# Paged sample attention: two groups of pages in flight, K and V pages requested in alternating runs of four

## The reference: what is computed

```
def fox_sample(k_past, v_past, logf_past, q, k, v, logf):
    ...
    s_past = jnp.einsum('bqhd,bkhd->bhqk', q, k_past).astype(F32) * scale + g[..., :, None] + suffix[..., None, :]
    s_new = jnp.einsum('bqhd,bkhd->bhqk', q, k).astype(F32) * scale + g[..., :, None] - g[..., None, :]
    ...
    p = jax.nn.softmax(jnp.concatenate([s_past, s_new], axis=-1), axis=-1).astype(v.dtype)
    return (jnp.einsum('bhqk,bkhd->bqhd', p[..., :n_past], v_past)
            + jnp.einsum('bhqk,bkhd->bqhd', p[..., n_past:], v))
```

## Time and profile before

| | |
|---|---|
| median of three executions | 2553.26 us (2551.98 to 2556.07) |
| profiled execution | 2555.88 us, span 2554.0 us |
| busy in the span | PE 2039.9 us, PEld 1529.0, DVE 1094.5, ACT 321.0, POOL 197.4 |
| DMA over the span | 320.44 MB, mean 125 GB/s |
| mean granted TensorE clock | 0.886 of full speed |

### The profile page before, as it was taken

The page is one execution under the profiler, slowest core; times in us unless marked ns, Lnnn a source line. Parts: engine busy times, 40 slices in busy tenths (PEclk is TensorE's granted clock), DMA queues, the critical chain, the costliest instruction groups (busy, mean ns, idle before and its releaser), DMA issues.

```text
span 2554.0 us, 41115 instructions
## 1 busy us (share of the span) xinstructions
PE 2039.9 (80%) x16723; PEld 1529.0 (60%) x16723; DVE 1094.5 (43%) x1979; ACT 321.0 (13%) x785; POOL 197.4 (8%) x266
## 2 busy tenths in 40 slices
PE   6998865455555555555899999999999889999996
PEld 4776643333333333334677777777777667777774
DVE  4323644444444444445443344533234543335443
ACT  2003520000000000000112210011110111220002
POOL 1003100000000000000100012220000110002221
PEclk9998987777667677677999999999999899999998
DMA  4121037677676777764111221231110111212211
GB/s 145 66 95 61 1 127 254 243 241 255 224 257 224 246 246 243 248 237 162 66 66 66 73 93 66 82 114 35 66 68 28 51 66 69 97 66 75 91 66 37
DMA packets 127992, 320.44 MB, mean 125 GB/s; under 512 B 10236, under 2 KB 10514, under 8 KB 127678
## 3 DMA queue, kind: packets, MB, share of 16 engines
q1 hardware_dynamic: 124258, 304.67, 33.8%
q0 software_dynamic: 3296, 12.98, 1.5%
q10 hardware_dynamic: 252, 0.16, 0.0%
HBM read 309.20 MB, written 8.55 MB: 124 GB/s over the span
## 4 chain that ended last, share of the span: by engine, by line
PE 78%; DVE 17%; ACT 2%; issue 2%; DMA 0%; DVEq 0%; ACTq 0%; SPq 0%
PE ps L852 44%; DVE work L1879 9%; PE ps L1052 8%; PE ps L1074 5%; PE ps L1149 2%; PE ps L1150 2%; PE ps L1062 2%; DVE stats L1894 2%; ACT work L1450 2%; PE ps L774 1%; PE ps L775 1%; PE ps L1001 1%; PE ps L803 1%; PE ps L804 1%; DVE work L1904 1%
## 5 line engine op out<-in xcount | busy, mean ns | idle before, releaser
L1052 PE MATMUL ps<-work,big 32*32 32x256 f32 x6144 | 191.7, 556 | 256.5 <-DVE work L1879 252.7
L1052 PEld LDWEIGHTS ps<-work,big 32*32 32x32 f32 x6144 | 133.8, 129 | 312.8 <-DVE work L1879 266.5
L852 PE MATMUL ps<-xn,wring 128*128 128x288 f32 x1104 | 295.8, 412 | 20.0 <-DVE xn L1598 15.7
L852 PE MATMUL ps<-work 128*128 128x288 f32 x1152 | 296.4, 411 | 11.9 <-DVE work L1645 7.8
L852 PEld LDWEIGHTS ps<-work 128*128 128x128 f32 x1152 | 222.0, 193 | 75.0 <-issue 12.8
L852 PEld LDWEIGHTS ps<-xn,wring 128*128 128x128 f32 x1104 | 212.1, 192 | 80.6 <-issue 20.1
L852 PE MATMUL ps<-big,wring 128*128 128x288 f32 x944 | 252.8, 412 | 7.6 <-DVE big L2142 7.6
L1879 DVE STREAM_TRANSPOSE work<-work 128x768 f32<-128x768 f32 x256 | 222.5, 935 | 0.0
L852 PEld LDWEIGHTS ps<-big,wring 128*128 128x128 f32 x944 | 182.2, 193 | 59.4 <-DVE big L2142 8.5
L1672 DVE TENSOR_TENSOR work<-ps,work 128x288 f32<-128x288 f32 x72 | 32.9, 457 | 320.5 <-PE ps L852 320.5
L707 POOL TENSOR_TENSOR h<-h,xn 128x288 f32<-128x288 f32 x96 | 106.0, 1107 | 812.6 <-DVE xn L1679 698.1
(11 more groups left out here) (348 smaller groups left out, 2507.9 us busy)
## 6 DMA issues: line engine op xcount, KB each, us to landing
work<-in_cache_k SPq DMA_DIRECT2D x256, 384.0 KB, 5.6
big<-in_cache_v SPq DMA_DIRECT2D x256, 384.0 KB, 5.4
wring<-in_w_up SPq DMA_DIRECT2D x16, 2048.0 KB, 7.5
wring<-in_w_down SPq DMA_DIRECT2D x16, 2048.0 KB, 7.9
wring<-in_w_in_odd SPq DMA_DIRECT2D x6, 2048.0 KB, 8.0
wring<-in_w_in_even SPq DMA_DIRECT2D x5, 2048.0 KB, 13.8
wring<-in_w_out_even SPq DMA_DIRECT2D x2, 2048.0 KB, 7.9
wring<-in_w_out_odd SPq DMA_DIRECT2D x2, 2048.0 KB, 7.9
```

The costliest lines, as they stand in the source:

```text
L852: last = mm(bank, w[:, k, :], x[:, k, :], start=k == 0 and not onto, stop=k == 3, skip_group_check=onto)
L1052: last = mm(ps[32 * c:32 * c + 32, 4 + q, 0:256], w, x, start=(n == 0), stop=(n == 2 * HC))
```

## The change

The work of a group is unchanged; its order on the engines, one PSUM area and the engine of one copy are not.

- SP requests K pages 0 to 7, and from there on runs of four K pages and four V pages in turn: K pages n to n+3, then V pages n-8 to n-5. The page numbers of both runs are read ahead of the K run. What each request waits for is the same as before.
- PE scores group g, then weighs pages 4 to 7 of group g-1, turns the probabilities of group g with eight transposes in a row (`turn_probs`), and weighs pages 0 to 3 of group g. The turned probabilities go to columns 256 to 511 of banks 4 to 7, beside the scores.
- ACT takes all eight turned tiles to SBUF with one copy of 128x1024 (`take_probs`), in place of DVE's two copies of 128x512.
- DVE turns the K pages of group g+1 while group g is worked on: three of them, then the shift of group g, one more, `add_out` of group g-1, the bias, and the last four.
- The new tokens' steps are split (`score_new`, `turn_new`, `weigh_new` on PE; `shift_new`, `take_new`, `start_out` on DVE) and spread over two groups; they and the turned output have areas of their own in bank 2. The counters `turn_taken` and its formulas are gone; the row sum and the decay have two slots, by the group's parity.

The diff, cut to its core:

```diff
         shift_s = lambda b, n: stat(b, 2 + n % 2)
-        den_s, group_den, decay, group_max, rec_s = (lambda b, n=n: stat(b, n) for n in (4, 5, 6, 7, 8))
+        den_s, group_max, rec_s = (lambda b, n=n: stat(b, n) for n in (4, 7, 8))
+        group_den, decay = (lambda g, n=n: stat(g // GS, n + 4 * (g % 2)) for n in (5, 6))
         c1 = work[:, 0:I["tab1"].shape[1]]
         O1 = I["tab1"].shape[1]
...
+        new_psum = ps[:, 2, 0:192]
+        out_psum = ps[:, 2, 192:448]
...
-            for g in range(NG):
-                for n in range(g * GP, (g + 1) * GP):
...
+            def k_page(n, page):
+                if n == 8:
+                    sp.wait_ge(sem("pool_d_ready"), 1)
+                if n >= KSLOTS:
+                    sp.wait_ge(sem("scored"), (n - KSLOTS) // GP + 1)
+                sp.dma_start(k_ring[:, k_slot(n), :], rows_of("cache_k", page)).then_inc(k_in[k_slot(n)], 16)
+            def v_page(n, page):
+                if n >= VSLOTS:
+                    sp.wait_ge(sem("v_page_used"), n - VSLOTS + 1)
+                sp.dma_start(v_ring[:, n % VSLOTS, :], rows_of("cache_v", page)).then_inc(v_in[n % VSLOTS], 16)
+            for n in range(0, GP, 4):
+                ids = page_ids(n)
+                for m in range(4):
+                    k_page(n + m, ids[m])
+            for n in range(GP, NB * PAGES, 4):
+                k_ids, v_ids = page_ids(n), page_ids(n - GP)
+                for m in range(4):
+                    k_page(n + m, k_ids[m])
+                for m in range(4):
+                    v_page(n - GP + m, v_ids[m])
+            for n in range(NB * PAGES - GP, NB * PAGES, 4):
+                ids = page_ids(n)
+                for m in range(4):
+                    v_page(n + m, ids[m])
...
-            def turn_half(g, u):
-                if u == 0:
-                    pe.wait_ge(sem("exp_done"), g + 1)
-                pe.wait_ge(sem("turn_taken"), turns_before_group(g) + u)
-                for m in range(4):
-                    at = place(g, 4 * u + m) * P
-                    last = tr(ps[:, 2, m * P:(m + 1) * P], probs[:, at:at + P], ident)
+            def turn_probs(g):
+                pe.wait_ge(sem("exp_done"), g + 1)
+                if g:
+                    pe.wait_ge(sem("probs_in"), g)
+                for at in range(GP):
+                    last = tr(ps[:, 4 + at // 2, 256 + at % 2 * P:256 + at % 2 * P + P], probs[:, at * P:at * P + P],
+                              ident)
                 last.then_inc(sem("probs_turned_s"), 1)
             def weigh_page(g, p):
                 n = g * GP + p
-                if p % 4 == 0:
-                    pe.wait_ge(sem("probs_in"), 2 * g + p // 4 + 1)
                 if p == 0:
-                    pe.wait_ge(sem("out_added"), outs_before_group(g))
+                    pe.wait_ge(sem("probs_in"), g + 1)
+                    if g:
+                        pe.wait_ge(sem("out_added"), g)
                 pe.wait_ge(v_in[n % VSLOTS], 16 * (n // VSLOTS + 1))
...
+            def score_new(b):
...
-                pe.wait_ge(sem("turn_taken"), turns_before_new(b))
+                if b:
+                    pe.wait_ge(sem("new_added"), b)
...
+            def turn_new(b):
...
+            def weigh_new(b):
...
             def turn_out(b):
...
+                if b:
+                    pe.wait_ge(sem("outputs_placed"), b)
+                tr(out_psum[:, 0:P], ostage[:, 0:P], ident)
+                tr(out_psum[0:D, P:2 * P], ostage[:, P:HC * D], ident).then_inc(sem("out_turned"), 1)
-            new_tokens(0)
+            score_new(0)
+            turn_new(0)
+            weigh_new(0)
             for g in range(NG):
+                b, new = g // GS, g // GS + 1
                 score_group(g)
-                if g % GS == 0 and g:
-                    turn_out(g // GS - 1)
-                for u in range(2):
-                    turn_half(g, u)
-                for p in range(GP):
+                if g:
+                    for p in range(GP // 2, GP):
+                        weigh_page(g - 1, p)
+                if g % GS == GS - 1 and new < NB:
+                    weigh_new(new)
+                turn_probs(g)
+                if g % GS == GS - 2 and new < NB:
+                    score_new(new)
+                for p in range(GP // 2):
                     weigh_page(g, p)
-                if g % GS == GS - 2 and g // GS + 1 < NB:
-                    new_tokens(g // GS + 1)
+                if g % GS == GS - 2 and new < NB:
+                    turn_new(new)
+                if g % GS == 0 and b:
+                    turn_out(b - 1)
+            for p in range(GP // 2, GP):
+                weigh_page(NG - 1, p)
             turn_out(NB - 1)
...
                 act.wait_ge(sem("shift_made"), g + 1)
                 if g:
-                    act.wait_ge(sem("probs_turned_s"), 2 * g)
+                    act.wait_ge(sem("probs_turned_s"), g)
                 act_f(probs.rearrange("p (g q k) -> p q g k", g=GP, q=4),
                       ps[:, 4:8, 0:256].rearrange("p q (g k) -> p q g k", g=GP), ACT.Exp,
-                      bias=shift_s(b, n), accum_out=group_den(b)).then_inc(sem("exp_done"), 1)
-                act_f(decay(b), shift_s(b, n - 1), ACT.Exp, bias=shift_s(b, n), scale=-1.0)\
+                      bias=shift_s(b, n), accum_out=group_den(g)).then_inc(sem("exp_done"), 1)
+                act_f(decay(g), shift_s(b, n - 1), ACT.Exp, bias=shift_s(b, n), scale=-1.0)\
...
+            def take_probs(g):
+                act.wait_ge(sem("probs_turned_s"), g + 1)
+                act_f(pTs.rearrange("p (a g) r -> p a (g r)", g=2), ps[:, 4:8, 256:512], ACT.Copy)\
+                    .then_inc(sem("probs_in"), 1)
             exp_new(0)
             for g in range(NG):
                 exp_group(g)
...
-            def take_half(g, u):
...
             def add_out(g):
                 b = g // GS
                 dve.wait_ge(sem("decay_made"), g + 1)
-                own(stt(den_s(b), den_s(b), decay(b), group_den(b), ALU.mult, ALU.add))
+                own(stt(den_s(b), den_s(b), decay(g), group_den(g), ALU.mult, ALU.add))
                 dve.wait_ge(sem("v_page_used"), GP * (g + 1))
-                dve.wait_ge(sem("out_added"), outs_before_group(g))
+                dve.wait_ge(sem("out_added"), g)
                 o = out_acc[:, b % 2, :]
-                stt(o, o, decay(b), ps[:, 3, 0:HC * D], ALU.mult, ALU.add).then_inc(sem("out_added"), 1)
...
+            def shift_new(b):
...
+            def take_new(b):
...
+            def start_out(b):
...
+            def turn_pages(g, pages):
+                if g < NG:
+                    for p in pages:
+                        turn_page(g * GP + p)
+            stage_queries(0)
+            shift_new(0)
+            take_new(0)
+            start_out(0)
+            turn_bias(0)
+            turn_pages(0, range(GP))
             for g in range(NG):
-                turn_bias(g)
-                for p in range(GP):
-                    turn_page(g * GP + p)
-                if g % GS == 0 and g:
-                    place_out(g // GS - 1)
+                b, new = g // GS, g // GS + 1
+                with_new = new < NB
+                if g % GS == GS - 2 and with_new:
+                    stage_queries(new)
+                turn_pages(g + 1, range(0, 3))
                 shift_group(g)
-                for u in range(2):
-                    take_half(g, u)
-                add_out(g)
-                if g % GS == GS - 1:
-                    scale_out(g // GS)
-                if g % GS == GS - 2 and g // GS + 1 < NB:
-                    new_tokens(g // GS + 1)
+                turn_pages(g + 1, range(3, 4))
+                if g:
+                    add_out(g - 1)
+                if g % GS == 0 and b:
+                    scale_out(b - 1)
+                if g % GS == GS - 1 and with_new:
+                    start_out(new)
+                if g + 1 < NG:
+                    turn_bias(g + 1)
+                if g % GS == GS - 2 and with_new:
+                    shift_new(new)
+                turn_pages(g + 1, range(4, 6))
+                if g % GS == GS - 2 and with_new:
+                    take_new(new)
+                turn_pages(g + 1, range(6, 8))
+                if g % GS == 0 and b:
+                    place_out(b - 1)
+            add_out(NG - 1)
+            scale_out(NB - 1)
```

More of the change, by code:

```diff
@@ L548, in rows_of @@
                 return I[cache][0, bass.ds(page, 1)].rearrange("o p h d -> (o p) (h d)")
-            for g in range(NG):
-                for n in range(g * GP, (g + 1) * GP):
-                    if n % 4 == 0:
-                        ids = page_ids(n)
-                    if n == 8:
-                        sp.wait_ge(sem("pool_d_ready"), 1)
-                    if n >= KSLOTS:
-                        sp.wait_ge(sem("scored"), (n - KSLOTS) // GP + 1)
```

(24 more changed lines are left out.)

44 lines of the change are left out of this document (8 added, 36 removed).

## The result

The changed kernel takes 2295.28 us (median of 4; 2289.08 to 2297.59), the kernel before beside it 2554.0 us. The ratio is 0.898 (95% interval 0.896 to 0.900), 259 us less. The forecast was 2278 us, within 2238 to 2350.

The account below looks back on a forecast made before the run. A chain of waits through one group was taken to bound the kernel. 31 steps of 17.0 us in place of 803.3 us save 276.3, plus 1 at the end, less 2.6 to the median: 2278 us, range 2238 to 2350.

Parts of the forecast that it names:

- What bounds the kernel: Sample attention: engines half busy, each waiting for the one ahead in the same group; 803.3 us for 31 steps, 25.91 each.
- Transfers, 15.7 us: Page transfers of one group: 6.29 MB at the 399 to 411 GB/s seen with full queues, 15.7 us.
- The rival that took 350 GB/s from the share: Page transfers: sustained rate below the burst, 350 GB/s at a full DMA share, 18.0 us a group; chance 0.24.
- PE's path, 14.9 us: PE in one group: 13.2 us busy, 0.4 exposed before turned tiles, 1.3 for ACT's copy and handoffs; 14.9 us.
- The request chain, 15.5 to 17.3 us: From one group's scores through requesting, landing and transposing the next K pages to its scores: 15.5 us, 17.3 with loaded queue.
- The sum, 17.0 us: One step of the loop: five paths side by side holding each other up, between 15.7 and 18.8 us, taken as 17.0.
- The allowance of 1.3 us above the transfers: Step of the loop: 1.3 us added to 15.7 us because the paths leave no room for each other's jitter.
- Starved PE: PE in scoring: instructions arrive late over the full DMA engines, 2.2 us a group more, step 19.2 us, 2346 us; chance 0.18.
- Transfers alone: Step of the loop: nothing but page transfers counts, 15.7 us a step, 2238 us; chance 0.12.
- the serial ring: SP's request order makes the loop serial again, 27.8 us a step, 2613 us; chance 0.04, including an overlap not coming about.

Follow-up runs that it names:

- the transfers almost alone: Changed kernel without K transposes (one column copied), scoring 32 of 112 products a group, weighing one product in most pages; all requests and waits kept: 2234.5 us.
- SP's old order: Changed kernel with all 8 K pages of a group requested, then all 8 V pages, compute order new: 2619.6 us, 1.027 of the kernel before.

## Why the prediction was right, point by point

**What bounds the kernel.** A chain through one group, with the stage's 803 us as all that can change: right. 265.7 of 266.8 us come from the stage.

**Transfers, 15.7 us.** 15.8 us at 397 GB/s with the transfers almost alone. The Trainium skill's page "DMA: Bandwidth & Descriptors", section Specifications, has 358 GB/s for a core, which would have made it 17.6 us; with one core at work, a stage of 490 us at 397 GB/s shows that it does not hold here. The rival that took 350 GB/s from the share would have been believed from the changed kernel's profile alone, 0.97 of the share at 360 GB/s; it was the better forecast of the number (2309 against 2278, measured 2295) for a reason that does not exist. A DMA share in the profile that is full by time in packets is not full by bytes.

**PE's path, 14.9 us.** With PE's wait for K pages left out: 11.4 busy, 1.0 for the exponential (0.4 forecast), 1.0 for the copy (1.3), 2.2 for instructions (none): 15.6 us. It did not bind: in all 31 steps the scores began within 0.1 us of the end of the last transpose. Two errors of about 2 us cancel. I had carried PE's busy time over at the old clock, and it fell from 13.2 to 11.4 us; and I had given late instructions to a rival.

**The request chain, 15.5 to 17.3 us.** This is what set the step. It measured 17.46 us in the changed kernel, at the top of its range. The landing was well bounded, 8.5 us against 7.0 with an empty queue and 8.8 with a loaded one. The scores are luck: forecast 7.3 and measured 7.7, they are made of 5.6 us of work, for which the old clock and one long group had stood (the mean of the kernel before was 6.8), and 2.1 us of late instructions, for which the sum had nothing. With a quarter of each page the scores took 5.65 us, the chain was no longer closed, and the step was 15.15 us.

**The sum, 17.0 us.** Measured 17.46, 14 us more over 31 steps, less 3.3 at the start and 1.5 at the tail (forecast 1 longer, measured 0.5 shorter): 9.5 us, and the profiled execution is 8.5 us over the 2280.6 forecast for it. It was the fastest of the four; the median is 17 us over the forecast. The allowance of 1.3 us above the transfers is 1.7. Its mechanism was right in the main: SP stops for `scored`, 1.8 us a step, the K run behind that stop lands late, and both other limits, 15.8 us for the transfers and 15.15 us with a quarter of the bytes, are well under 17.46. What was missing are the late instructions. How much of the 1.7 is theirs was not isolated: no run had full transfers and full compute without them. The 31 steps of the changed kernel give an estimate. The 7 with under 0.5 us of late instructions took 16.5 us on average, the other 24 took 17.7, and a straight line through all has 0.25 us of step for each us of lateness (standard error 0.07), 0.7 us for the mean of 2.7. The delay is not passed on whole; when the scores take longer, the K pages behind them tend to land sooner. One figure of the prediction is off by itself: steps of 16.4 to 17.5 us are 2260 to 2294 us by its own sum, not 2262 to 2296, because the 2.6 us to the median were left out there. The forecast and the range are not touched by it.

**The rivals.** Starved PE (19.2 us a step, 0.18) had a mechanism that is there. Its 2.2 us a step is what the waits view has; that it would come on top of 17.0 was wrong, since PE's path without it is 13.4 us and not 14.9, and its scores 5.6 and not 7.3. The Trainium skill's page "Runtime: NRT & Kernel Launch", section Instruction fetch mechanics, has fetching hidden behind issue; the 27 waits here are a case where it isn't. Transfers alone (15.7) and the serial ring did not come; a ring of that kind came in SP's old order.

## What to carry to other kernels

When all engines are half busy, lay the waits of one group end to end, and bound each resource for itself before believing that an overlap will hold; here the transfers, SP, PE and the request chain were each put at about 15 to 16 us, and the step is 17.5. Then measure the links of the chain in the new trace too: the waits view alone made PE's path look like the limit, and two experiments that shortened or moved ACT's copy changed next to nothing. A pipeline over an in-order request queue needs both orders at once: the requests must stand in the order in which their waits are met, or the first one that can't be met stops those that could be, and each half of the change alone loses 2.7%. When one engine issues tens of instructions a microsecond beside full DMA queues, look for waits put down to issue, and see whether they end a fixed time behind an instruction packet.

## What the runs showed of the hardware that was not expected

- Instructions for PE came late by up to 4.0 us beside the page transfers, 27 times, and 12 times by at most 1.5 us at a quarter of the bytes (70.1 against 11.1 us in 480). PE went on 1.4 us (medians 1.35 to 1.5) after the packet's end in all kernels that had such waits. With a third of the weight loads in a step and the queues full at 397 GB/s there was none: it takes both, the rate of use and the load.
- A DMA share of 0.97 went with 360 GB/s in one kernel and a share of 1.02 with 395 in another, with the same packets.
- A K transpose took 0.935 us in the kernel before and 0.97 us on average behind the change. It goes with whether DVE had stood idle: all 73 that began after such a wait took 0.978 to 0.980 us, and 0.977 to 0.979 in the run with a quarter of the bytes (59). The 146 of the kernel before, none of them behind a wait, took 0.933 to 0.939. Those behind the change that began without a wait lie anywhere from 0.926 to 0.980; the cause stays open.
